# Experts' gate and up projections as three fp32r passes with the gathered rows loaded, weights split on chip, down one expert later, seven weight slots instead of eight

## The reference

```python
act = jax.nn.silu(jnp.einsum('bnd,edf->bnef', h, w_g)) * jnp.einsum('bnd,edf->bnef', h, w_u)
out = jnp.einsum('bnef,efd->bnd', act * comb.astype(act.dtype)[..., None], w_d)
```

## Time and profile before

| | us |
|---|---|
| median of 3 runs | 1385.43 |
| lowest and highest | 1383.98, 1385.45 |
| the profiled execution's own time | 1385.98 |
| span of its trace | 1384.0 |
| PE busy | 1319.9 (95% of the span) |
| DVE busy | 821.4 (59%) |
| ACT busy | 407.8 (29%) |
| POOL busy | 471.4 (34%) |

### The profile page before, as it was taken

The page is one execution under the profiler, slowest core; times in us unless marked ns, Lnnn a source line. Parts: engine busy times, 40 slices in busy tenths (PEclk is TensorE's granted clock), DMA queues, the critical chain, the costliest instruction groups (busy, mean ns, idle before and its releaser), DMA issues.

```text
span 1384.0 us, 21022 instructions
## 1 busy us (share of the span) xinstructions
PE 1319.9 (95%) x7647; PEld 1108.3 (80%) x7647; DVE 821.4 (59%) x2051; ACT 407.8 (29%) x916; POOL 471.4 (34%) x769
## 2 busy tenths in 40 slices
PE   5999999999989999998999999999999979999986
PEld 5978999999979999995555555899788848888852
DVE  5454778889999988816666555343556632222226
ACT  5554222122121122224555433110322212222213
POOL 4800595878872126540000000120011223232314
PEclk9999999999999999999999899999999989999998
DMA  7201232222213231002000221743301058999847
GB/s 249 70 24 42 75 82 78 39 72 56 63 56 111 65 98 46 1 24 73 1 16 1 64 64 33 281 152 134 148 31 41 36 200 322 396 344 338 304 188 312
DMA packets 71117, 163.76 MB, mean 118 GB/s; under 512 B 12529, under 2 KB 38721, under 8 KB 69873
## 3 DMA queue, kind: packets, MB, share of 16 engines
q1 hardware_dynamic: 56929, 129.31, 26.9%
q0 software_dynamic: 12656, 27.62, 6.0%
q10 hardware_dynamic: 1440, 5.58, 1.0%
HBM read 137.81 MB, written 39.21 MB: 128 GB/s over the span
## 4 chain that ended last, share of the span: by engine, by line
PE 90%; POOL 3%; DVE 2%; ACT 2%; DMA 1%; issue 1%; ACTq 0%; POOLq 0%; SPq 0%; DVEq 0%
PE bank L768 11%; PE bank L769 11%; PE bank L770 11%; PE bank L1126 8%; PE bank L955 5%; PE bank L919 4%; PE bank L1132 4%; PE bank L942 3%; PE bank L1026 3%; PE bank L1020 3%; PE bank L890 2%; PE bank L1038 2%; PE bank L1037 2%; PE bank L1039 2%; PE bank L1119 2%; PE bank L980 2%
## 5 line engine op out<-in xcount | busy, mean ns | idle before, releaser
L1602 DVE MAX8 small<-region_kv 128x8 f32<-128x272 f32 (+4 forms) x241 | 190.2, 828 | 51.3 <-DVE region_kv L1607 51.2
L768 PE MATMUL bank<-h_hi,w_hi 128*128 128x384 f32 (+1 forms) x576 | 196.1, 341 | 0.0
L769 PE MATMUL bank<-h_lo,w_hi 128*128 128x384 f32 (+1 forms) x576 | 196.1, 340 | 0.0
L1607 DVE MATCH_REPLACE8 region_kv<-small,region_kv 128x272 f32<-128x272 f32 (+4 forms) x241 | 195.5, 818 | 0.0
L770 PE MATMUL bank<-h_hi,w_lo 128*128 128x384 f32 (+1 forms) x576 | 194.4, 338 | 0.0
L1889 POOL TENSOR_TENSOR w_lo<-w_stage,w_hi 128x512 fp32r<-128x512 f32 x64 | 80.8, 1297 | 149.5 <-ACT w_hi L1210 149.4
L768 PE MATMUL bank<-w_hi,h_hi 128*128 128x256 f32 x448 | 129.9, 290 | 1.4 <-ACT region_q L1270 1.4
L770 PE MATMUL bank<-w_hi,h_lo 128*128 128x256 f32 x448 | 125.9, 281 | 0.0
L769 PE MATMUL bank<-w_lo,h_hi 128*128 128x256 f32 x448 | 125.8, 281 | 0.0
L770 PEld LDWEIGHTS bank<-h_hi,w_lo 128*128 128x128 f32 x576 | 108.7, 189 | 0.0
L769 PEld LDWEIGHTS bank<-h_lo,w_hi 128*128 128x128 f32 x576 | 108.2, 188 | 0.6
(11 more groups left out here) (273 smaller groups left out, 2818.5 us busy)
## 6 DMA issues: line engine op xcount, KB each, us to landing
w_stage<-in_w_in SPq DMA_DIRECT2D x72, 256.0 KB, 3.2
region_kv<-in_xa SPq DMA_DIRECT2D x16, 512.0 KB, 5.7
region_q<-in_wg SPq DMA_DIRECT2D x12, 512.0 KB, 8.8
region_q<-in_wu SPq DMA_DIRECT2D x12, 512.0 KB, 20.3
region_q<-in_wd SPq DMA_DIRECT2D x12, 512.0 KB, 22.4
region_h<-in_wg SPq DMA_DIRECT2D x12, 512.0 KB, 10.9
region_h<-in_wu SPq DMA_DIRECT2D x12, 512.0 KB, 20.3
region_h<-in_wd SPq DMA_DIRECT2D x12, 512.0 KB, 23.5
```

Of the source, the lines that this page charges most:

```text
L768: mm(out, st_hi(k), mv_hi(k), start=(k == 0), stop=False)
L769: mm(out, st_hi(k), mv_lo(k), start=False, stop=False)
L1602: nc.vector.max(m8[:, q, :], x).then_inc(dve_c, 1)
L1607: nc.vector.match_replace(x, m8[:, q, :], x, TAKEN).then_inc(dve_c, 1)
```

## The change

Gate and up of an expert become 24 fp32r matmuls with 256 moving columns (`gate_up_split`): the loaded operand is now a piece of the transposed rows (`rowsT_hi` or `rowsT_lo`), the moving one gate and up side by side (`e_high`, the high part, or `e_rest`, the rest). So the result has rows as partitions; the product with silu goes to `act_rows`, PE turns it (`turn_act`), ACT copies it to `actT`, and `down` follows one expert later (`down_of(e - 1)` in turn e). The weights are split on the chip: ACT casts gate and up of expert e+2 (`expert_upper`), DVE subtracts (`expert_lower`), in place in the slot. The rows are split as they leave PSUM: ACT casts (`rows_upper`), DVE subtracts (`rows_lower`). ACT takes over one half of scaling the down result (`second_half`), DVE keeps the other (`first_half`); the scatter waits for both. There are seven weight slots. The lines that the three new buffers need stand left out in this cut:

```diff
         eslot = ([RW[:, 0:3072], RW[:, 3072:6144]] + [RQ[:, 3072 * i:3072 * i + 3072] for i in range(3)]
-                 + [RH[:, 3072 * i:3072 * i + 3072] for i in range(3)])
+                 + [RH[:, 3072 * i:3072 * i + 3072] for i in range(2)])
...
                     if u >= 2:
                         pe.wait_ge(te_evac, u - 1)
+                        pe.wait_ge(rows_low, u - 1)
...
+            def gate_up_split(e):
...
+                pe.wait_ge(wao_high, 3 * KD + 2 * e + 2)
+                pe.wait_ge(wao_low, 3 * KD + 2 * e + 2)
+                pe.wait_ge(te_evac, 2 * e + 2)
+                if e >= 2:
+                    pe.wait_ge(act_ready, e - 1)
+                for k in range(KD):
+                    mm(out, rowsT_hi[:, par, k, :], high[:, :, k, :], start=(k == 0), stop=False, skip_group_check=True)
+                    mm(out, rowsT_hi[:, par, k, :], rest[:, :, k, :], start=False, stop=False, skip_group_check=True)
+                pe.wait_ge(rows_low, 2 * e + 2)
+                for k in range(KD):
+                    last = mm(out, rowsT_lo[:, par, k, :], high[:, :, k, :], start=False, stop=(k == KD - 1),
+                              skip_group_check=True)
+                last.then_inc(gu_done, 1)
...
             for e in range(NE):
...
+                gate_up_split(e)
                 if e + 1 < NE:
                     e_trans(e + 1)
...
+                if e >= 1:
+                    down_of(e - 1)
+                turn_act(e)
+            down_of(NE - 1)
...
             for e in range(NE):
...
+                act.wait_ge(gu_done, e + 1)
+                if e >= 2:
+                    act.wait_ge(act_ready, e - 1)
+                silu_e(e % 2)
+                if e + 1 < NE:
+                    rows_upper(e + 1)
+                if e + 2 < NE:
+                    expert_upper(e + 2)
+                act.wait_ge(act_turned, e + 1)
...
+                cp(actT[:, e % 2, :], bank[6 + e % 2][:, 2 * P:3 * P]).then_inc(actT_ready, 1)
+                if e >= 1:
+                    second_half(e - 1)
...
                 pool.wait_ge(y_ready, e + 1)
+                pool.wait_ge(y_act, e + 1)
                 scatter(ysb[:, e % 3, :], heads[:, e, 0:1], y_out[e % 3])
```

More of the change, by code:

```diff
@@ L94, in build @@
             w_out_hi = out_weights_hi.enter_context(nc.sbuf_tensor("w_out_hi", [P, KD, D], F32R))
+        e_rest = [None] * 7
+        with ExitStack() as slots_q:
+            for q in range(2, 5):
+                e_rest[q] = slots_q.enter_context(nc.sbuf_tensor(f"expert_rest{q}", [P, 2, KD, P], F32R))
+                slots_q.enter_context(nc.sbuf_tensor(f"down_of_slot{q}", [P, D], F32))
         RQ = sb("region_q", [P, 9216])
@@ L128, in build @@
             stage_t = sb_early("w_stage", [P, 4 * 512], F32)
+        with ExitStack() as slots_h:
+            for q in range(5, 7):
+                e_rest[q] = slots_h.enter_context(nc.sbuf_tensor(f"expert_rest{q}", [P, 2, KD, P], F32R))
+                slots_h.enter_context(nc.sbuf_tensor(f"down_of_slot{q}", [P, D], F32))
+            rowsT_lo = slots_h.enter_context(nc.sbuf_tensor("rowsT_lo", [P, 2, KD, P], F32R))
         RH = sb("region_h", [P, 9344])
@@ L1134, in down, with turn_act, down_of @@
                 last.then_inc(dn_done, 1)
+            def gate_up_split(e):
+                par = e % 2
+                out = bank[6 + par][:, 0:2 * P]
+                rest, high = e_rest[e % NSLOT], e_high[par]
+                pe.wait_ge(wao_high, 3 * KD + 2 * e + 2)
[11 more added lines that the diff above has]
+                last.then_inc(gu_done, 1)
+            def turn_act(e):
+                pe.wait_ge(act_ready, e + 1)
+                nc.tensor.transpose(bank[6 + e % 2][:, 2 * P:3 * P], act_rows[:, e % 2, :], ident).then_inc(act_turned, 1)
+            def down_of(e):
+                pe.wait_ge(actT_ready, e + 1)
+                if e >= 2:
+                    pe.wait_ge(y_ready, e - 1)
+                    pe.wait_ge(y_act, e - 1)
+                down(e % NSLOT, e % 2)
             pe.wait_ge(x2_ready, 2 * NT)
@@ L1488, in _ @@
             for e in range(NE):
[L1489 to L1494, removed]
-                           bank[4 + hf][:, :].rearrange("p (k t) -> p k t", k=4)).then_inc(te_evac, 1)
-                    act.wait_ge(gu_done, e + 1)
-                    if e >= 2:
-                        act.wait_ge(act_ready, e - 1)
-                    silu_e(e % 2)
+                act.wait_ge(gu_done, e + 1)
@@ new lines, in rows_lower, with first_half @@
+            def rows_lower(e):
+                for hf in range(2):
+                    dve.wait_ge(te_evac, 2 * e + hf + 1)
+                    ks = slice(4 * hf, 4 * hf + 4)
+                    tt(rowsT_lo[:, e % 2, ks, :], bank[4 + hf][:, :].rearrange("p (k t) -> p k t", k=4),
+                       rowsT_hi[:, e % 2, ks, :].bitcast(F32), ALU.subtract).then_inc(rows_low, 1)
+            def first_half(y):
+                dve.wait_ge(dn_done, y + 1)
+                if y >= 3:
+                    dve.wait_ge(y_out[y % 3], 16 * (y // 3))
+                ts(ysb[:, y % 3, 0:512], bank[2 * (y % 2)][:, :], pos_w[:, y, 1:2], None, ALU.mult).then_inc(y_ready, 1)
@@ new lines, in _ @@
+            expert_lower(0)
+            expert_lower(1)
+            rows_lower(0)
+            for e in range(NE):
+                dve.wait_ge(silu_done, e + 1)
+                if e >= 2:
+                    dve.wait_ge(act_turned, e - 1)
+                tt(act_rows[:, e % 2, :], silu[:, e % 2, :], bank[6 + e % 2][:, P:2 * P], ALU.mult).then_inc(act_ready, 1)
+                if e + 1 < NE:
+                    rows_lower(e + 1)
+                if e >= 1:
+                    first_half(e - 1)
+                if e + 2 < NE:
+                    expert_lower(e + 2)
@@ L1832, in _ @@
+            first_half(NE - 1)
             dve.wait_ge(over_in, 32)
```

69 lines of the change are left out of this document (48 added, 21 removed).

## The result

The changed kernel takes 1419.09 us in the median (1415.33 to 1428.28, four runs) against 1385.18 (1383.98 to 1385.45, four runs): a ratio of 1.0265, 95% interval 1.024 to 1.029. The forecast was 1392 us with a range of 1378 to 1408. The direction was right; the loss is 34 us where 7 were expected.

A forecast was written before the change was run, and what follows sets the result against it. PE (6.24 us per expert) and weight transfers (6.36) were taken as close to balance, with gathers deciding afterwards. First turns -2.5, other experts +8.4, end +0.5 on 1386.0 gave 1392.4, median 1392 us; range 1378 to 1408.

The forecast's parts named there:

- PE's turn: Expert stage: PE's work per expert falls from 6.24 to 5.63 us, 0.61 less.
- all of PE's gain: Far end of the rival that PE, not transfers, sets the expert stage's pace: 1366 us; rival's chance 0.16.
- The gather loop: Expert stage: rows gathered behind POOL's late scatter are needed two turns later, so two turns equal 6.9 us plus gather latency.
- The way: Expert stage: time from the start of an expert's transposes to the issue of the gather behind them, 6.9 us.
- The landing: Expert stage: time from a gather's issue until its rows are there, 8.6 us median before, 4.5 shortest, expected between.
- L: The gather's latency in the expert stage: 5.8 us keeps a 6.36 us turn, the middle is 6.55.
- T: Length of one expert's turn after the change: 6.55 us taken, between 6.36 and 6.73; +8.4 us over 27 experts.
- The first turns: Start of the expert stage: four turns at 5.63 us with rows and weights ahead, -2.5 us.
- The stretch of POOL's issue: DVE's weight subtractions might lengthen POOL's gather or scatter issue: up to 12 us, left out of the sum, in the range.
- the one of full latency: Rival in the expert stage: gathers keep full latency and POOL's issues are stretched, 1407 to 1424 us; chance 0.13.
- The clock: Rival: the clock falls because PE idles about 0.9 us of 6.5 in the expert stage; little chance.
- The transfers: Expert stage: weight loads come at 6.36 us an expert because the transfers allow no more.

The follow-up runs named there:

- without the rests: Changed kernel without DVE's subtractions for the experts' weights from expert 2 on (output differs): 1417.79 us, ratio 1.024.
- no loads: Changed kernel without the weight loads of experts 7 to 31 (output differs): 1378.13 us, ratio 0.9959.
- Filling two gaps: Changed kernel with seven filler matmuls ahead of the wait for the gathered rows of expert 4 and of expert 6: 1422.81 us, ratio 1.0280.
- the early gather: Changed kernel with each gather one scatter earlier in GpSimd's queue, three turns to land instead of two: 1384.05 us, ratio 0.9998.
- the kernel before with less PE: Kernel before the change with 12 of the 16 gate and up matmuls per expert (output differs): 1377.46 us, ratio 0.9956.
- four kernels: Changed kernel (1419.09 us), and it with ACT's second half before weight casts (1418.80), without weight rests (1417.79), or with loads issued behind the gather (1422.02).

## Why the prediction was right in direction and wrong in size

- **PE's turn, right.** 5.63 us was worked out from the earlier trace rows; 5.57 is measured where nothing else holds it, and the 1366 us put down for "all of PE's gain" are 1365.19. ACT and DVE are not the pace, as said from the earlier trace rows.
- **The gather loop, right.** Its shape (two turns = way + landing), the releaser (ACT's second half), the idle time ahead of the transposes, SP's wait for the down matmul: all stand in the trace. The way was put at 6.9 us and is 7.05 to 7.2, in part by luck: 0.47 us of it are the stretch of the scatter's issue, which the sum left out, and without the rests the way is 6.6 to 6.7.
- **The landing, the term that failed.** I took L near 6.2, half way between the value for the load pace and the middle of the earlier trace rows, because "each us that the gathers cost PE lets the queue drain". It does, from a share of 0.95 to 0.84, and the landing falls from 8.6 only to 7.4. That gives T = 7.2 where 6.55 was summed. At 6.55 the DMA engines would still move 95% of what they moved at 6.24; no row supported a landing 2.4 us shorter for so little relief. The two ends, 4.5 and 8.6, were good (no loads gave 4.4); the choice between them was not. From expert 8 to 23 this step is worth 10.4 us.
- **The first turns, wrong.** Four turns were to run at 5.63 on rows and weights loaded ahead. "Ahead" held for weights and not for rows: three gathers are ahead, but that of expert 4 already hangs on the scatter of expert 0 and was issued at 1149.10. From the transposes of expert 4 to those of 8, 35.5 us, the chain has two ways of 9.6 and 7.8 us and two landings of 9.7 and 8.4, where the sum has 6.9 and 6.2 for each. The first way is so long above all because transposes and down ran at half clock, a term that was put at nothing. In all the first eight turns are 13.1 us over the sum, more than the landing costs later.
- **The sum by stretches,** on the profiled run, which is 24.7 us above the 1392.4 of the sum: experts 0 to 3, +1.2 instead of -2.5, 3.7 us; 4 to 7, 4 x (8.9 - 6.55) = 9.4; 8 to 23, 16 x (7.2 - 6.55) = 10.4; the rest of the experts 0.5 and the end 0.5. That is 24.5.
- **The stretch of POOL's issue, right as a fact and worthless as a price.** The row of 1.87 us, beside a scalar_tensor_tensor, spoke against the rule of the Trainium skill, SBUF — State Buffer, section "Who interferes with whom", that writing descriptors is not held up by tensor_tensor (inferred there). Here the scatter took 1.48 us beside such instructions and 1.01 without them, so the trace does not agree with the rule. But 12 us as the price of it rested on a landing of fixed length, and that fell.
- **The rival that came true** is the one of full latency, 1407 to 1424 us, at 0.13. Its own condition, L of 7.3 or more, was met, but only just: the landing did not keep its 8.6 us. At T = 7.2 its formula gives 1410 us for the profiled execution; that 1417.07 came out is mostly due to the first eight turns, which it had no more than the forecast. So its price was right in part by luck. Its "against" was the argument that sank the sum.
- **The clock, wrong.** It was dismissed for gaps of 0.9 us; the gaps are 2 to 5 us and the clock was 0.76 in 1160 to 1180. Filling two gaps gave 2 us of four turns back; what the falls cost in the rest of the stage is not shown.
- **The transfers, right.** 6.36 us per expert from the earlier trace rows as what the loads allow: 6.1 us with the early gather, 6.5 in the kernel before with less PE. The Trainium skill, DMA: Bandwidth & Descriptors, section "The descriptor swizzle", led to an estimate of 6.4; the runs lie on both sides of it, and none of them tells the engines apart, so they neither show nor refute the spreading.

## What to carry to other kernels

When a result is produced one iteration later, follow every in-order queue that waits for it and look for a prefetch behind that wait: the order "gather, then scatter" was harmless at one distance and cost 34 us at the next, and moving the gather one place gave all of it back. Where a wait closes a loop through a shared resource, don't take a landing half way between loaded and unloaded, but ask what share of the engines stays busy at the new pace: here it was still 7.4 of 8.6 us at a share of 0.84. And before making an engine quicker, take work off it in the kernel before: one such run showed here that 30 us less of PE is worth 6.5.

## What the hardware did that I had not expected

- The landing of a gather followed the end of the down matmul at 11.5 us in four kernels whose gathers left 3.3 to 4.3 us after it and whose loads stood before or behind it. That it is so is shown; why two changes so different leave it alone is open. With the DMA engines at 0.94 to 0.95 it followed the issue instead, at 8.6 to 8.8 us.
- Two subtractions on DVE with both inputs in SBUF made an indirect DMA's issue on GpSimd 1.48 us (scatter) and 2.04 us (gather) long, against 1.01.
- Around the end of idle times of 4.6 and 5.2 us of PE the granted clock was at half, 1.2 GHz, for 6.8 us each time, and the transposes behind them took 1.97 us instead of 1.04.
